# First attention tile of a conv + attention + MoE trunk: the second tile's expert sum moves behind the K/V product and half of Q, and the rows of the third and fourth tiles are gathered once the query weights are there

## The chip, the cores and the metric

One core of one Trainium2 chip runs the whole kernel. The metric is the device time of one execution in microseconds (us), lower is better.

## The reference

The kernel computes two decoder layers over 512 tokens of width 1024, all in float32 (batch 1):

```
layer 0:  x = LN(ALPHA*x + conformer_conv(x))          # 31-wide causal depthwise conv between two products
          x = LN(ALPHA*x + grouped_moe(x))             # 16 experts, top 2 of one group, 1024 -> 512 -> 1024
          k, v = rope(x @ kv_w[:, :256] + ..), x @ kv_w[:, 256:] + ..   # 4 kv heads of 64
layer 1:  q = rope(x @ wq + bq)                        # 16 heads of 64
          x = LN(ALPHA*x + (softmax(q k^T / 8, window 128, one sink a head) v) @ wo + bo)
          x = LN(ALPHA*x + grouped_moe(x))
```

The experts' results are weighted with two gates a token and added to the token's row: `y = sum of gate_j * expert_j(x)`, j = 0, 1.

## The kernel before, in words

The 512 tokens are 4 tiles of 128 tokens (`T = 4`), a tile being [128 partitions x 1024]. The program is written for each engine by hand: a list of instructions that runs in its written order, with semaphores between the lists. Five lists matter here: PE (matrix products and transposes), DVE (vector work, reads the products), ACT (copies out of PSUM, exponentials, and a DMA queue), POOL (`rstd`, the residual, and all indirect DMAs) and SP (the weights' DMA queue).

Between the experts of layer 0 and the attention, each tile goes through the same steps ("combine" in DVE's list, L1499):

- POOL gathers the tile's expert results from DRAM (`xs_dram`), two indirect DMAs of 128 rows of 4 KB each into `yg[l][t][0..1]` (L2102; semaphore `s_yg[t]`, 32 when both have landed). `yg_slots` (L216) says which weight slots hold these rows.
- ACT scales the first of the two with its gate, in place (`gated_y`, L1860, semaphore `s_y0g`).
- DVE adds the second, scaled, to `x` (L1510), adds the first (L1513), and makes the layer norm: statistics (L1215 to L1218, semaphore `s_mv`), a scaling (L1252), and after POOL's `rstd` (`inverse_std`, L2036, one instruction) the last step (L1259, semaphore `s_ln`). `s_ln` reaches `T + 1` when tile 0 is done and `T + 2` when tile 1 is. Tile 0 uses a slightly different sum (L1476, L1482) and no `gated_y`.

The attention runs over the tiles 0 to 3. Its work is cut in units, named kind and tile, which PE makes (`unit`, L1009) and ACT or DVE take (`take`): Xa and Xb are the two halves of the tile's transpose (PE L1024, taken by ACT L1882), KV, Q0 and Q1 the products with the K/V weights and the two halves of the query weights (PE L1032, 16 matmuls each), KT, QTa and QTb the transposes of K and of the two halves of Q. For KV, Q0 and Q1, DVE adds the bias and rotates (L1531 to L1536, L1575 to L1586). W0 and W1 are the output products (PE L1051). Every engine goes through the units in one written order: `first_units` (L408) is Xa, Xb, KV, Q0, Q1, KT, QTa of tile 0, and then for each tile four steps, one for each kv head. In a step stand: the scores (PE L1079), softmax in DVE (`soft`: L1613 to L1624), ACT's exponentials (`exps`: L1892, L1894, eight and one), the normalisation (`normed_probs`: DVE L1631 to L1634), PE's transpose of the probabilities (L1091), ACT's copy (L1904), and the product with V (PE L1105). Between these PE makes the units of the next tile. In the first step of tile 0 the order is, on PE: scores, Xa(1), Xb(1), QTb(0), KV(1), scores of the next head, transposes of the probabilities; on ACT: Xa(1), Xb(1), the exponentials, QTb(0), ...; on DVE: `soft`, combine of tile 2, `normed_probs`, KV(1), ... Tile 3 is combined in the first step of tile 1.

SP loads the K/V weights in slot 0, the query weights in slots 1 and 2 (`s_wq[0]`, `s_wq[1]`), then waits for the last gathered rows (`s_yg[T - 1]`) and for `s_ln`, and loads the output weights in slots 3 and 4. Before the change, the rows of tile 0 lie in the first half of slot 3, those of tile 1 in slot 6 (a part of `arena`, which also holds K and V of the attention), and those of tiles 2 and 3 in slot 5.

The 56 transposes of the identity at L617 do nothing for the result. They fill PE's wait for tile 0.

POOL's list after the layer 0 experts (L2088):

```
for t in range(T):
    if l == 0 and t == 1:
        inverse_std(n)
        for b in range(2):
            pool.wait_ge(s_y[b], 32 * 8)          # the last two experts' rows are in DRAM
    for j in range(2):
        pool.indirect_dma_start(out=yg[l][t][j], ...)
for t in range(l == 0, T):
    inverse_std(n + t)
```

Of the kernel before, what the change touches and what calls it, by code (L numbers as in the profile page):

```python
# [31 lines left out]
T = S // P  # L32
# [49 lines left out]
def trunk(nc, x_in, positions, conv_w1, conv_b1, conv_dw, conv_dwb, conv_ln_g, conv_ln_b,  # L82
# [14 lines left out]
    with ExitStack() as ctx:  # L97
# [3 lines left out]
        def sem(name):  # L101
            return ctx.enter_context(nc.semaphore(name))
# [110 lines left out]
        hT = [view(AT + 1536, 2, P), view(AT + 1792, 2, P), view(8192, 2, P)]  # L213
        slots = [wring[:, i, :] for i in range(6)] + [view(EARLY, KD * F), view(LATE, KD * F), aux[:, 2 * D:6 * D]]
        ring_order = [[1, 2, 3, 6, 7, 4, 5, 0], [5, 0, 1, 2, 3, 4, 6, 7]]
        yg_slots = [((3, 0), (6, 0), (5, 0), (5, 1)), ((7, 0), (7, 1), (5, 0), (5, 1))]  # L216

        QUARTERED = ((1, 4), (1, 5))

# [25 lines left out]
        SUMMED = (1, T)  # L245
# [52 lines left out]
        s_ln = sem("s_ln")  # L298
# [58 lines left out]
        s_wq = [sem(f"s_wq{i}") for i in range(2)]  # L357
# [126 lines left out]
        def _(sp):  # L484
# [36 lines left out]
            def consumed(l, m):  # L521

                e, kind = divmod(m, 3)
                sp.wait_ge(s_dn if kind == 2 else s_gud, E * l + e + 1)
# [37 lines left out]
            sp.dma_start(slot(2, KD), wq_src[:, :, 512:1024]).then_inc(s_wq[1], 16)  # L562
            sp.wait_ge(s_yg[T - 1], 32)
            consumed(0, 3 * E - 5)
            sp.wait_ge(s_ln, T + 1)
            sp.dma_start(slot(3, KD), wo_src[:, :, 0:512]).then_inc(s_wo[0], 16)
            consumed(0, 3 * E - 2)
            sp.dma_start(slot(4, KD), wo_src[:, :, 512:1024]).then_inc(s_wo[1], 16)
# [574 lines left out]
        def _(dve):  # L1143
# [199 lines left out]
            n = 0  # L1343
# [155 lines left out]
            def combine(l, n, tiles):  # L1499

                for t in tiles:
                    if t == 0:
                        add_far(l)
                        add_kept(l)
                        dve.wait_ge(s_rows2, 16 * 2)
                        norm_x(t, n + t, l, 1)
                        continue
                    y0, y1 = yg[l][t]
                    dve.wait_ge(s_yg[t], 32 * (l + 1))
                    own(dve.scalar_tensor_tensor(out=x_sb[:, t, :], in0=y1, scalar=gate_w[:, 1, t:t + 1],  # L1510
                                                 in1=x_sb[:, t, :], op0=ALU.mult, op1=ALU.add))
                    dve.wait_ge(s_y0g, t - SUMMED[l] + 1)
                    dve.tensor_tensor(x_sb[:, t, :], x_sb[:, t, :], y0, ALU.add).then_inc(s_cmb, 1)  # L1513
                    dve.wait_ge(s_cmb, t - SUMMED[l] + 1)
                    norm_x(t, n + t, l, 1)

            experts(0)
            combine(0, n, range(2))
            n += T


# [37 lines left out]
            def take(u, n):  # L1559

                kind, t = u
                if kind == "E":
                    if t == T - 1:
                        bank = full(dve, u)
                        unscaled_logits(1, n + t, ps[:, bank, 0:E], bank_read[bank - 5])
                        first_picks(1, T - 2)
                    route(1, t)
                    return
                if kind[0] in "XDP" or kind in ("KT", "QTa", "QTb") or u == ("R", T - 2):
                    return  # L1570
                bank = full(dve, u)
                if kind == "KV":
                    if t >= 1:
                        full(dve, ("KT", t - 1))
                    dve.tensor_tensor(v_sb[:, t, :], ps[:, bank, KVD:2 * KVD], kvrow[:, KVD:2 * KVD], ALU.add)  # L1575
                    dve.tensor_tensor(k_sb, ps[:, bank, 0:KVD], kvrow[:, 0:KVD], ALU.add
                                      ).then_inc(bank_read[bank - 5], 1)
                    taken(dve, u)
                    own(rotate(t, k_sb.rearrange("p (h d) -> p h d", h=NKV), NKV,
                               (kr[:, :, 0, 0:HH], kr[:, :, 0, HH:HD]), tk))  # L1580
                    dve.tensor_copy(kr[:, :, 1, :], kr[:, :, 0, :]).then_inc(s_kr, 1)
                elif kind in ("Q0", "Q1"):
                    h = int(kind[1])
                    if t >= 1:
                        full(dve, ("QT" + "ab"[h], t - 1))
                    dve.tensor_tensor(q_sb, ps[:, bank, :], bqrow[:, h * 512:(h + 1) * 512], ALU.add  # L1586
                                      ).then_inc(bank_read[bank - 5], 1)
                    taken(dve, u)
                    part = qr[:, 8 * h:8 * h + 8, :]
                    rotate(t, q_sb.rearrange("p (h d) -> p h d", h=8), 8,  # L1590
                           (part[:, :, 0:HH], part[:, :, HH:HD]), tq).then_inc(s_qr, 1)
                elif kind in ("W0", "W1"):
                    h = int(kind[1])
                    dve.wait_ge(s_xb, t + 1)
                    half_x = x_sb[:, t, h * 512:(h + 1) * 512]
                    dve.scalar_tensor_tensor(out=half_x, in0=half_x, scalar=ALPHA, in1=ps[:, bank, :],
                                             op0=ALU.mult, op1=ALU.add).then_inc(bank_read[bank - 5], 1)
                    if h == 1 and t == T - 1:
                        norm_tile(t, n)
                else:  # L1600
                    places(1, t, bank)
                    first_picks(1, t)
# [32 lines left out]
                                  ).then_inc(s_pn, 1)  # L1635

            for u in first_units:
                take(u, n)
            for t in range(T):
                soft(t, 0)  # L1640
# [27 lines left out]
        def _(act):  # L1668
# [18 lines left out]
            for r in range(ROUNDS):  # L1687
                n = min(SHIFTS, CW - SHIFTS * r)
# [171 lines left out]
            def gated_y(l, t):  # L1860

                y0 = yg[l][t][0]
                act.wait_ge(s_yg[t], 32 * (l + 1))
                act.activation(y0, y0, ACT.Copy, scale=gate_w[:, 0, t:t + 1]).then_inc(s_y0g, 1)
# [20 lines left out]
            def exps(t, kh):  # L1885
                m = NKV * t + kh
                lo = 0 if t else P
                act.wait_ge(s_negm, m + 1)
                gq = slice(kh * GQ, (kh + 1) * GQ)
                for i in range(GQ):  # L1890
                    h = kh * GQ + i
                    act.activation(pr[m % 2][:, i, lo:256], pr[m % 2][:, i, lo:256], ACT.Exp,  # L1892
                                   bias=negm[:, h:h + 1], accum_out=den[:, h:h + 1])
                act.activation(exs[:, 1, gq], exs[:, 0, gq], ACT.Exp).then_inc(s_ex, 1)  # L1894
# [19 lines left out]
            for i, u in enumerate(first_units):  # L1914
                take(u)
                if i == 1:
                    for t in range(SUMMED[0], T):
                        gated_y(0, t)
            act.dma_start(resrow, attn_bo[0].partition_broadcast(P)).then_inc(s_rows3, 16)
            norm_rows(1, s_rows3)  # L1920
            for t in range(T):
                for kh, (early, late) in enumerate(fillers(t)):
                    if kh:
                        exps(t, kh)
                    for u in early:
                        take(u)
                    if kh == 0:
                        exps(t, 0)
                    if kh:
                        keep_o(t, kh - 1)  # L1930
                    for u in late:
                        take(u)
                    keep_pt(t, kh)
                    if t == T - 1 and kh < 2:
                        permuted(1, kh)
                if t == T - 1:
                    for u in last_units[0:3]:
                        take(u)
                keep_o(t, NKV - 1)
# [15 lines left out]
        def _(pool):  # L1955
# [78 lines left out]
            def inverse_std(n):  # L2034
                pool.wait_ge(s_mv, n + 1)
                pool.tensor_tensor(rstd[:, n:n + 1], vareps[:, n:n + 1], half[:, :], ALU.pow).then_inc(s_rs, 1)  # L2036
# [51 lines left out]
            def combine(l, n):  # L2088
                stored = in_register(pool, r_pool, pool.snap(g, min_val=1, max_val=4096) * (16 * QUADS))
                for b in range(2):  # L2090
                    pool.wait_ge(s_y[b], 32 * (8 * (l + 1) - l - (l == 0)))
                if l == 0:
                    pool.wait_ge(s_gud, E - 1)
                pool.wait_ge(s_oy, stored)

                for t in range(T):
                    if l == 0 and t == 1:
                        inverse_std(n)
                        for b in range(2):
                            pool.wait_ge(s_y[b], 32 * 8)  # L2100
                    for j in range(2):
                        pool.indirect_dma_start(out=yg[l][t][j], out_offset=None, in_=xs_dram[:, :],  # L2102
                                                in_offset=bass.IndirectOffsetOnAxis(ap=place_i[:, j, t:t + 1], axis=0)
                                                ).then_inc(s_yg[t], 16)
                for t in range(l == 0, T):
                    inverse_std(n + t)

            def number_kept():
# [64 lines left out]
```

## Time and profile before

| | |
|---|---|
| median of 3 runs | 1044.74 us (1037.29, 1044.74, 1045.21) |
| the profiled execution | 1046.18 us, of which the span of the profile is 1044.5 us |
| busy in the span | PE 936.1 us (90%), DVE 455.1, ACT 182.8, POOL 191.4 |
| mean granted TensorE clock | 0.969 of full |
| moved by DMA | 308.71 MB, 296 GB/s over the span |

The profile is of one execution. Times in it are us from the start of the span. The page cuts the span in 40 slices of 26.1 us, and gives the busy share in tenths for each engine and for the 16 DMA engines. The stretch that the change touches is from 500 to 580 us, the 20th to 23rd slice. All sums are made against the profiled execution.

### The profile page before, as it was taken

The numbers are of one execution on the slowest core, as the hardware profiler recorded it, in microseconds if no ns is written. First come the engines' busy times: TensorE is split into PE (matmuls) and PEld (weight loads), VectorE is DVE, ScalarE is ACT, GpSimd is POOL, SyncE is SP. The second block draws the span as 40 slices with busy tenths as digits, with TensorE's granted clock in tenths as the row PEclk, the third lists the DMA queues.
The fourth block names the chain that finished last, engine by engine and source line by source line (L and its number), as shares of the span: only waits on it lengthen the run. The fifth ranks groups of instructions, "written<-read, shape, count | busy, mean of one in ns | idle before, by whom it ended". The sixth has DMA issues, their size and how long they took to land.

```text
span 1044.5 us, 15695 instructions
## 1 busy us (share of the span) xinstructions
PE 936.1 (90%) x6044; PEld 500.4 (48%) x6044; DVE 455.1 (44%) x915; ACT 182.8 (17%) x398; POOL 191.4 (18%) x319
## 2 busy tenths in 40 slices
PE   6999989999999689979989899989999878998994
PEld 4444444557454345534534444454665444544541
DVE  4799983454121011111377586658512211121136
ACT  0100031242111001000032423346311000100100
POOL 1230021023312022100300031002132112212031
PEclk9999999899999899999999899998999989999998
DMA  9995279987999999999880022405879999999982
GB/s 286 376 410 205 72 251 393 378 326 301 365 359 386 396 390 393 391 401 410 325 336 1 1 81 81 161 1 202 300 277 389 371 400 407 371 417 382 416 326 89
DMA packets 75352, 308.71 MB, mean 296 GB/s; under 512 B 9519, under 2 KB 21723, under 8 KB 59130
## 3 DMA queue, kind: packets, MB, share of 16 engines
q1 hardware_dynamic: 37344, 230.32, 57.5%
q10 hardware_dynamic: 27930, 51.14, 13.2%
q0 software_dynamic: 9984, 25.97, 6.9%
q8 instruction: 63, 1.03, 0.4%
q14 instruction: 31, 0.25, 0.1%
HBM read 250.33 MB, written 53.74 MB: 291 GB/s over the span
## 4 chain that ended last, share of the span: by engine, by line
PE 56%; DMA 17%; DVE 15%; issue 7%; ACT 2%; POOL 1%; ACTq 0%; SPq 0%; POOLq 0%; DVEq 0%
PE ps L827 17%; DVE arena L1201 8%; PE ps L837 8%; DMA wring<-in_moe_w_gate_dram 6%; PE ps L722 6%; PE ps L847 4%; DMA arena<-in_moe_w_gate_dram 3%; PE ps L1032 3%; DMA wring<-in_moe_w_up_dram 3%; PE ps L649 3%; PE ps L1051 3%; DMA wring<-in_attn_wq_dram 3%; PE ps L857 2%; PE ps L610 1%; PE ps L1002 1%
## 5 line engine op out<-in xcount | busy, mean ns | idle before, releaser
L827 PE MATMUL ps<-wring,arena 128*64 128x256 f32 x1504 | 177.6, 391 | 24.6 <-DMA wring<-in_moe_w_gate_dram 15.8
L827 PEld LDWEIGHTS ps<-wring,arena 128*64 128x64 f32 x1504 | 109.9, 140 | 86.6 <-DMA wring<-in_moe_w_gate_dram 18.7
L649 PE MATMUL ps<-arena,wring 128*128 128x512 f32 x256 | 110.4, 593 | 1.4 <-DVE arena L1159 1.4
L1407 DVE COPY arena<-ps 128x256 f32<-128x256 f32 x32 | 13.6, 425 | 219.1 <-PE ps L941 202.4
L1201 DVE SCALAR_TENSOR_TENSOR arena<-arena,dwT 128x512 f32<-128x512 f32 x145 | 102.3, 780 | 0.0
L1032 PE MATMUL ps<-wring,arena 128*128 128x512 f32 x192 | 86.3, 604 | 7.0 <-DMA wring<-in_attn_wq_dram 4.0
L837 PE MATMUL ps<-wring,arena 128*64 128x512 f32 x384 | 86.5, 592 | 0.0
L2050 POOL DMA_DIRECT2D arena<-xs_dram x112 | 59.7, 540 | 117.7 <-DVE arena L1386 80.4
L649 PEld LDWEIGHTS ps<-arena,wring 128*128 128x128 f32 x256 | 48.5, 190 | 61.9 <-issue 60.3
L827 PE MATMUL ps<-arena 128*64 128x256 f32 x544 | 65.9, 397 | 9.5 <-DMA arena<-in_moe_w_gate_dram 9.5
L2036 POOL TENSOR_TENSOR rstd<-vareps,half 128x1 f32<-128x1 f32 x20 | 23.8, 1189 | 265.4 <-DVE vareps L1218 265.4
L722 PE MATMUL ps<-wring,arena 128*128 128x512 f32 x128 | 61.3, 634 | 0.5 <-DVE x_sb L1266 0.5
L1032 PEld LDWEIGHTS ps<-wring,arena 128*128 128x128 f32 x192 | 36.2, 193 | 50.2 <-issue 49.3
L1799 ACT ACTIVATE arena<-ps 128x512 f32<-128x512 f32 x32 | 19.1, 597 | 215.4 <-PE ps L837 215.4
L827 PEld LDWEIGHTS ps<-arena 128*64 128x64 f32 x544 | 40.1, 143 | 34.1 <-DMA arena<-in_moe_w_gate_dram 11.5
L1401 DVE TENSOR_TENSOR arena<-arena,ps 128x256 f32<-128x256 f32 x32 | 13.4, 420 | 87.9 <-PE ps L827 87.9
L837 PEld LDWEIGHTS ps<-wring,arena 128*64 128x64 f32 x384 | 27.5, 137 | 45.2 <-issue 41.9
L1051 PE MATMUL ps<-wring,arena 128*128 128x512 f32 x96 | 42.5, 595 | 0.0
L1417 DVE TENSOR_TENSOR arena<-arena,ps 64x256 f32<-64x256 f32 x14 | 5.9, 424 | 79.6 <-ACT arena L1820 79.6
L847 PE MATMUL ps<-wring,arena 128*32 128x256 f32 x608 | 40.2, 380 | 0.0
L722 PEld LDWEIGHTS ps<-wring,arena 128*128 128x128 f32 x128 | 25.3, 204 | 29.9 <-issue 28.9
L2075 POOL COPY arena<-arena 128x256 f32<-128x256 f32 x14 | 5.6, 401 | 177.4 <-DMA arena<-xs_dram 115.7
(251 smaller groups left out, 1145.0 us busy)
## 6 DMA issues: line engine op xcount, KB each, us to landing
wring<-in_moe_w_gate_dram SPq DMA_DIRECT2D x23, 2048.0 KB, 25.0
wring<-in_moe_w_up_dram SPq DMA_DIRECT2D x23, 2048.0 KB, 19.5
wring<-in_moe_w_down_dram SPq DMA_DIRECT2D x23, 2048.0 KB, 22.9
xs_dram<-zero ACTq DMA_DIRECT2D x2, 16384.0 KB, 50.3
arena<-in_moe_w_gate_dram SPq DMA_DIRECT2D x9, 2048.0 KB
arena<-in_moe_w_up_dram SPq DMA_DIRECT2D x8, 2048.0 KB
arena<-in_moe_w_down_dram SPq DMA_DIRECT2D x6, 2048.0 KB
xs_dram<-arena ACTq DMA_DIRECT2D x60, 128.0 KB, 8.9
```

Source lines behind the costliest of these rows:

```text
L649: last = pe.matmul(ps[:, 2 * (c % 4) + h, :], w[:, k, h, (c % 2) * P:(c % 2) * P + P], xT[:, k, :], start=(k == 0), stop=(k == KD - 1))
L722: last = pe.matmul(ps[:, 4 + h, :], hc[t % 2][:, c, :], slot(4 + c // 4, 4)[:, c % 4, h * 512:(h + 1) * 512], start=(c == 0), stop=(c == K ...
L827: mm = pe.matmul(ps[h * CAP:(h + 1) * CAP, bank, 0:256], act[:, k, :], w[:, k, h * 256:(h + 1) * 256], start=(k == 0), stop=(k == KD - 1))
L837: mm = pe.matmul(ps[h * CAP:(h + 1) * CAP, bank, :], act[:, j % 2, (j // 2) * CAP:(j // 2 + 1) * CAP], w[:, j, h * 512:(h + 1) * 512], sta ...
L847: mm = pe.matmul(ps[q * XROWS:(q + 1) * XROWS, bank, 0:256], xgxT[:, k, :], gate_up[i][:, k, h * 256:(h + 1) * 256], start=(k == 0), stop= ...
L857: mm = pe.matmul(ps[q * XROWS:(q + 1) * XROWS, bank, 0:D // QUADS], hTx[:, at:at + XROWS], w[:, j, q * (D // QUADS):(q + 1) * (D // QUADS) ...
L1032: last = pe.matmul(ps[:, bank, :], xTt[:, k, :], slot(at, KD)[:, k, :], start=(k == 0), stop=(k == KD - 1))
L1051: last = pe.matmul(ps[:, bank, :], oT[t % 2][:, k, :], slot(3 + h, KD)[:, k, :], start=(k == 0), stop=(k == KD - 1))
L1201: dve.scalar_tensor_tensor(out=acc, in0=hpad[:, c, k:k + S], scalar=dwT[:, c, k:k + 1], in1=acc, op0=ALU.mult, op1=ALU.add).then_inc(s_tap, 1)
L1799: act.activation(ysb[b], ps[:, 4, :], ACT.Copy).then_inc(s_yc, 1)
L2036: pool.tensor_tensor(rstd[:, n:n + 1], vareps[:, n:n + 1], half[:, :], ALU.pow).then_inc(s_rs, 1)
L2050: pool.dma_start(where[q * QROWS:(q + 1) * QROWS, :, :], xs_tiles[q, :, bass.ds(n, 1), :, :]).then_inc(signal, 16)
```

## The change

Five edits, which hang together:

1. DVE combines tile 1 not before `first_units` but within them, after it has taken Q0 and before it takes Q1.
2. POOL issues the gathers of tile 1 as before, then makes tile 1's `rstd`, then waits until the second half of the query weights has landed (`s_wq[1]`), and only then issues the four gathers of tiles 2 and 3.
3. ACT scales tile 1's rows after Xb as before, but tile 2's after all of `first_units`, and tile 3's after the first exponentials of tile 0.
4. The rows of tile 1 are gathered to the second half of slot 3 in place of slot 6.
5. SP's load of the output weights into slot 3 waits for `s_ln` at `T + 2` (tile 1 done) in place of `T + 1`.

```diff
-        yg_slots = [((3, 0), (6, 0), (5, 0), (5, 1)), ((7, 0), (7, 1), (5, 0), (5, 1))]
+        yg_slots = [((3, 0), (3, 1), (5, 0), (5, 1)), ((7, 0), (7, 1), (5, 0), (5, 1))]
...
             consumed(0, 3 * E - 5)
-            sp.wait_ge(s_ln, T + 1)
+            sp.wait_ge(s_ln, T + 2)
             sp.dma_start(slot(3, KD), wo_src[:, :, 0:512]).then_inc(s_wo[0], 16)
...
             experts(0)
-            combine(0, n, range(2))
+            combine(0, n, range(1))
...
             for u in first_units:
+                if u == ("Q1", 0):
+                    combine(0, n - T, range(1, 2))
                 take(u, n)
...
             for i, u in enumerate(first_units):
                 take(u)
                 if i == 1:
-                    for t in range(SUMMED[0], T):
-                        gated_y(0, t)
+                    gated_y(0, 1)
+            gated_y(0, 2)
             act.dma_start(resrow, attn_bo[0].partition_broadcast(P)).then_inc(s_rows3, 16)
             norm_rows(1, s_rows3)
...
                     if kh == 0:
                         exps(t, 0)
+                        if t == 0:
+                            gated_y(0, 3)
...
                 for t in range(T):
+                    if l == 0 and t == 2:
+                        inverse_std(n + 1)
+                        pool.wait_ge(s_wq[1], 16)
                     if l == 0 and t == 1:
                         inverse_std(n)
...
-                for t in range(l == 0, T):
+                for t in range(2 if l == 0 else 0, T):
                     inverse_std(n + t)
```

## Rows read from the trace of the kernel before

**Rows 1.** The page: PE's busy time, and the DMA engines' share in 40 slices.

```profile
PE 936.1 (90%) x6044; PEld 500.4 (48%) x6044; DVE 455.1 (44%) x915; ACT 182.8 (17%) x398; POOL 191.4 (18%) x319
...
DMA  9995279987999999999880022405879999999982
```

**Rows 2.** The chain that ended last, from 496 us: start, us, what.

```profile
496.54 6.14 DMA wring<-xs_dram,place_i
...
503.79 27.40 DMA wring<-in_attn_wq_dram
```

**Rows 3.** Timeline of PE: start, us, line, instructions merged, idle before and its releaser.

```profile
513.40 13.11 PE L1032 MATMUL ps<-wring,arena 128*128 128x512 f32 x30 [0.77 <-ACT arena L1882]
...
524.63 2.74 PE L1032 MATMUL ps<-wring,arena 128*128 128x512 f32 x6
531.32 8.80 PE L1032 MATMUL ps<-wring,arena 128*128 128x512 f32 x16 [3.96 <-DMA wring<-in_attn_wq_dram]
...
544.56 7.10 PE L1032 MATMUL ps<-wring,arena 128*128 128x512 f32 x16 [0.43 <-ACT arena L1882]
...
553.41 0.66 PE L1091 MATMUL ps<-ident,arena 128*128 128x128 f32 x4 [1.10 <-DVE arena L1634]
...
602.15 7.13 PE L1051 MATMUL ps<-wring,arena 128*128 128x512 f32 x16
```

**Rows 4.** Windows: PE busy, granted clock, DMA share, GB/s.

```profile
527.00:529.00 2.00, 0.37 (x1) 1.00 1.04 410
529.00:531.00 2.00, 0.00 (x0) 1.00 0.35 138
...
533.00:535.00 2.00, 2.00 (x3) 0.50 0.81 272
...
582.00:584.00 2.00, 2.00 (x12) 0.52 0.00 0
```

**Rows 5.** Timeline of DVE, tile 1's sum to tile 0's first probabilities.

```profile
523.94 1.28 DVE L1510 SCALAR_TENSOR_TENSOR x_sb<-arena,gate_w,x_sb 128x1024 f32<-128x1024 f32 x1 [12.53 <-DMA arena<-xs_dram,place_i]
...
528.08 0.15 DVE L1218 TENSOR_SCALAR vareps<-mv 128x1 f32<-128x1 f32 x1
...
529.96 1.28 DVE L1259 SCALAR_TENSOR_TENSOR x_sb<-x_sb,rstd,aux 128x1024 f32<-128x1024 f32 x1 [0.53 <-POOL rstd L2036]
...
533.86 0.68 DVE L1586 TENSOR_TENSOR arena<-ps,aux 128x512 f32<-128x512 f32 x1
...
536.63 0.42 DVE L1536 TENSOR_TENSOR arena<-arena 128x256 f32<-128x256 f32 x1
...
543.28 0.68 DVE L1613 SCALAR_TENSOR_TENSOR arena<-ps,mask 128x512 f32<-128x512 f32 x1
...
545.07 1.28 DVE L1510 SCALAR_TENSOR_TENSOR x_sb<-wring,gate_w,x_sb 128x1024 f32<-128x1024 f32 x1
...
552.66 0.69 DVE L1634 TENSOR_TENSOR arena<-arena,rden 128x512 f32<-128x512 f32 x1
```

**Rows 6.** Timeline of POOL: tile 3's last gather, tile 1's rstd.

```profile
520.33 0.95 POOL L2102 DMA_INDIRECT wring<-xs_dram,place_i  x1 [0.30 <-issue]
528.32 1.53 POOL L2036 TENSOR_TENSOR rstd<-vareps,half 128x1 f32<-128x1 f32 x1 [7.04 <-DVE vareps L1218]
```

**Rows 7.** Timeline of ACT and its DMA queue (ACTq), up to the first exponentials.

```profile
531.67 1.15 ACT L1864 ACTIVATE wring<-wring,gate_w 128x1024 f32<-128x1024 f32 x1 [2.51 <-DMA wring<-xs_dram,place_i]
...
541.04 0.39 ACTq L1919 DMA_DIRECT2D aux<-in_attn_bo_dram  x1
...
541.93 0.45 ACTq L1696 DMA_DIRECT2D aux<-in_ln_b_dram  x1
543.22 1.08 ACT L1882 ACTIVATE arena<-ps 128x512 f32<-128x512 f32 x2 [1.54 <-PE ps L1024]
```

**Rows 8.** An indirect DMA's issue on POOL beside DVE work, in the last tile.

```profile
749.48 1.80 POOL L2044 DMA_INDIRECT xs_dram<-x_sb,place_i  x1 [0.96 <-DVE place_i L1317]
```

**Rows 9.** Timeline of DVE at that place.

```profile
749.10 1.28 DVE L1252 SCALAR_TENSOR_TENSOR x_sb<-x_sb,mv,aux 128x1024 f32<-128x1024 f32 x1
```

## The prediction

> **What bounds the kernel now.** The page comes first: PE is busy for 90% of the span, and the DMA engines are nearly full except in slices 21 to 26, the attention [rows 1]. So around 500 to 530 us two things are tight at once: PE waits for what it needs, and every byte in flight delays every other. The chain that ended last goes there from a gather (496.54 us, 6.14 us long) straight into the load of the second half of the query weights, issued at 503.79 and landed 27.40 us later, at 531.19 [rows 2]. PE's timeline shows what that costs: KV and Q0 of tile 0 run from 513.40 without a gap to 524.63 + 2.74 = 527.37, PE then stands still for 3.96 us, and Q1 takes 8.80 us where the same 16 matmuls take 7.10 at 544.56 [rows 3]. The windows say why: behind the gap the granted clock falls to 0.50, the lower of its two levels, 1.2 of 2.4 GHz [rows 4]. So the late weights cost 3.96 + 1.70 = 5.7 us at this place. From 544.56 the list goes on through KV(1), the scores and the transposes of the first probabilities at 553.41, which waited 1.10 us for DVE [rows 3]. After this point the four steps of each tile hang on one another through PE, DVE and ACT, and the expert weights of layer 1 are loaded as the attention frees its slots, into a DMA stream that is full to the end [rows 1]. I therefore carry a shift of 553.41 to the end one to one.
>
> **What the held-back gathers free.** Four gathers of 0.52 MB, 2.1 MB, leave the stream ahead of the query weights. At 410 GB/s, the rate just before the drain [rows 4], that is 5.1 us, so the weights land at about 526, before PE has finished Q0 at 527.4 (the drain itself, 410 then 138 GB/s, moves along). Q1 then starts at 527.4, at full clock, and ends at 534.5. The gain at this place is the 5.7 us from above.
>
> **What moves on DVE.** Tile 1's sum and norm take 523.94 to 529.96 + 1.28 = 531.24, 7.3 us, and the K/V unit follows, to 533.86, 2.6 us; the Q0 unit goes on to 536.63 + 0.42 = 537.05, 3.2 us [rows 5]. After the change the K/V unit lies under the Q0 product and costs nothing. The Q0 unit starts at 527.4 and ends at 530.6, tile 1's sum and norm end at 537.9, and the Q1 unit (3.2) ends at 541.1. The softmax of head 0, from 543.28 to 545.07 before [rows 5], can be over at 542.9. That is 2.2 us earlier. DVE's order alone has thus already eaten 3.5 of the 5.7 us. KT and QTa need only the K/V and Q0 units, so PE and ACT are through them some 3 us after 534.5.
>
> **Where the gathers go.** POOL now makes tile 1's rstd before it issues them, so they wait for DVE, not for the weights. From the start of tile 1's sum to its variance are 528.08 + 0.15 - 523.94 = 4.3 us [rows 5], and rstd takes 1.53 after a tenth [rows 6]: 530.6 + 4.3 + 1.6 = 536.5. The weights landed at 526, so that second wait is free. Issues cost 0.95 us and 0.30 between them [rows 6]. The first falls on DVE's last norm step (from 536.6, 1.28 us, two inputs in SBUF). The nearest row is the issue at 749.48, beside the same kind of step at 749.10: 1.80 us in place of 0.95 [rows 8, 9]. I take that for the first issue only: 536.8 to 538.6, second from 538.9. A second gather after a pause needed 6.14 us [rows 2], so tile 2's rows land at 538.9 + 6.1 = 545.0, tile 3's 2.5 us later. Bounds: with no slowing of the issue and a quicker landing 543.4; with both issues slowed and a landing a microsecond slower 547.
>
> The Trainium skill ("DMA: Bandwidth & Descriptors", the section on the anatomy of one DMA from GpSimd) gives about 2.0 us plus the bytes at 436 GB/s for such a DMA. By it the second gather would land some 4.2 us after its issue begins instead of 6.1, an estimate from its figures, and the sum below would be 1.9 us smaller. The row here is longer and decides. The skill's "SBUF — State Buffer" ("Who interferes with whom") says that a DVE instruction with two SBUF inputs and a GpSimd instruction that reads SBUF exclude each other for the whole of an instruction; the 1.80 us issue agrees, and taken literally, a blocked second issue would add up to about half a microsecond.
>
> **Who waits for tile 2's rows.** Two engines. ACT meets `gated_y(0, 2)` right after QTa, at about 537, and stands there until 545.0. Before, it scaled the last rows at 531.67, when it had nothing else to do [rows 7]. Behind it are queued the three DMA issues of the bias and norm rows (541.04 to 541.93 + 0.45 = 1.34 us), the copies Xa(1) and Xb(1) (1.08 us) [rows 7], and all exponentials. The issues run beside the scaling (1.15 us), so the copies start at 546.3 and end at 547.4, and PE can start KV(1) 0.26 us later, as it did at 544.56 after the copies' end at 544.30 [rows 3, 7]: at 547.7, which is 3.1 us later than before. PE itself is there long before. It has made Xa(1), Xb(1) and QTb(0) by 542 and has had little since 535. A wait like that costs clock: 4 us of standing still took 1.70 us from Q1 [rows 3, 4]. I take 1.7 here as well. KV(1) ends at 547.7 + 7.1 + 1.7 = 556.5, and with 0.7 for the scores (553.41 - 1.10 - 551.66) the transposes of the probabilities come at 557.2. The second waiter is DVE: tile 2's sum and norm start at 545.0 instead of 545.07 and so end when they did, and the probabilities are ready at 553.3 as before (552.66 + 0.69) [rows 5], 4 us before PE wants them. The 1.10 us that PE waited for them is gone.
>
> **The sum.** 557.2 - 553.4 = +3.8 us. In terms of the steps: +3.1 for KV(1)'s start, +1.7 clock, -1.1 for the wait that is absorbed, and 0.1 of rounding. The 5.7 us at Q1 are spent before KV(1), because KV(1) doesn't wait for Q1 any more but for ACT.
>
> **Edits with no cost.** Tile 3's rows (landed about 547.5) are scaled after the exponentials, about 550, 1.15 us more of ACT; the QTb copy behind it is wanted for the third head only. The output weights' loads move from 531.7 to about 547.5 and, 4.2 MB at 410 GB/s, land by some 558; the first product with them is at 602.15 [rows 3]. `s_ln` at `T + 2` comes at 537.9 and doesn't end that wait. The other half of slot 3 holds the same bytes as slot 6 would. Without that cover of over 40 us the load's 10 us would show in full; nothing here comes near.
>
> **The rivals.**
> (a) *The gathers are in time, faster.* If tile 2's rows landed before DVE is through head 0's softmax at 542.9, ACT would be free, and the transposes would start when DVE is ready, 2.2 us earlier than before. For: the gathers meet an empty DMA stream. Against: 542.9 leaves 4.0 us from the second issue, and no row shows a landing under 6. It gives 1042.6, and is the most that can be gained: DVE's order alone forbids more.
> (b) *Nothing reaches the end.* Any of the later waits (PE's wait for DVE at the end of tile 0, the full DMA stream of layer 1) takes up the shift: 1044.7. Against: both are started by the same list.
> (c) *The clock stays low, slower by over 1%.* Between 535 and 547 PE has only some 3 us of transposes and scores. In the sparse stretch after tile 0's last head the clock was still at 0.52 from 582 to 584 [rows 4]. If PE were at 1.2 GHz through KV(1) and the work after it, as long as each product only follows short waits, KV(1) and Q0(1) would cost 7.1 us more each in place of 1.7: +3.1 - 1.1 + 14.2 = +16 us, 1061. It decides from the point where a full product no longer brings the clock back; Q1's 8.80 us speak against it, since the clock was back within the product. With only KV(1) wholly slow it is +9.1, 1053.8.
>
> **How the numbers follow.** The profiled execution took 1046.18 us and the median is 1044.74; I put the shift on the median: 1044.7 + 3.8 = 1048.5. The forecast's own ends are 543.4 for the landing with no clock lost (KV(1) at 546.1, transposes at 553.9: +0.5, 1045.2) and 547 with 3.5 us of clock lost (+7.7, 1052.4). Chances: forecast 0.66, (a) 0.14, (b) 0.12, (c) 0.08, of which half stays within 1%. The runs of before lie 8 us apart (1037.29 to 1045.21), so about 1% (10.4 us) is what a measurement can tell from no change, and a median can fall low by itself; with that and (a) the low end is 1041, the high end 1053. Faster by over 1%: 0.03, for a low median on top of (a). Slower by over 1%: 0.06. Within 1%: 0.91.
>
> **What the profile after would show.** Right: Q1 of tile 0 starting at 527 to 528 with no wait and taking 7.1 us; POOL's four gathers from about 537; ACT's longest wait, 6 us or more, at L1864 for a DMA; KV(1) at 547 to 548, released by ACT's copy. Wrong: an ACT wait under 3 us there (then (a)), the gathers waiting for the weights rather than for rstd, PE still idle before Q1 (the stream isn't what held the weights), or KV(1)'s shift not found again in the start of layer 1's experts (then (b)).

## The result and the profile after

The changed kernel took 1050.32 us (median of 20 runs) against 1044.33 for the kernel before (20 runs): ratio 1.0048, 95% interval 1.0034 to 1.0063, or 5.0 us slower on 1044, between 3.6 and 6.6. (The two medians lie 6.0 us apart; what follows goes by the ratio and its interval.) The forecast was +3.8 us. Run again later beside the kernel before, the ratio was 1.0046 (1.0023 to 1.0069), and the kernel before against itself gave 0.9992 (0.9967 to 1.0018).

Every execution reaches the first KV product at another time (513.40 in the profile of before, 510.52 here), so the spans of two profiles, 1044.5 and 1045.6, can't be set against each other. I count from the start of that product instead, written as +.

PE's timeline after the change, to be read against [rows 3]:

```profile
510.52 20.84 PE L1032 MATMUL ps<-wring,arena 128*128 128x512 f32 x48 [0.78 <-ACT arena L1884]
...
533.06 0.71 PE L1079 MATMUL ps<-arena 64*128 64x128 f32 x8 [0.83 <-ACT arena L1884]
535.65 1.16 PE L1024 MATMUL ps<-ident,x_sb 128*128 128x128 f32 x8 [1.87 <-DVE arena L1586]
538.25 1.09 PE L1044 MATMUL ps<-ident,arena 128*128 128x128 f32 x4 [1.44 <-DVE arena L1536]
543.36 9.26 PE L1032 MATMUL ps<-wring,arena 128*128 128x512 f32 x16 [4.03 <-ACT arena L1884]
...
553.20 0.66 PE L1091 MATMUL ps<-ident,arena 128*128 128x128 f32 x4
```

KV, Q0 and Q1 are one row of 48 matmuls with no gap: the weights are there. Then PE waits four times, the last time and longest for ACT's copies before KV(1), which starts at +32.84 and takes 9.26 us instead of 7.1. The 1.10 us wait for DVE at L1091 is gone. ACT's timeline says why (its L1866 is the scaling, L1884 the copies), with its DMA queue's issues among it, against [rows 7]:

```profile
540.46 1.15 ACT L1866 ACTIVATE wring<-wring,gate_w 128x1024 f32<-128x1024 f32 x1 [7.54 <-DMA wring<-xs_dram,place_i]
540.46 0.39 ACTq L1921 DMA_DIRECT2D aux<-in_attn_bo_dram  x1
540.89 0.44 ACTq L1697 DMA_DIRECT2D aux<-in_ln_g_dram  x1
541.36 0.62 ACTq L1698 DMA_DIRECT2D aux<-in_ln_b_dram  x1
542.03 1.09 ACT L1884 ACTIVATE arena<-ps 128x512 f32<-128x512 f32 x2 [0.42 <-issue]
```

ACT stood 7.54 us for tile 2's rows; behind it the three issues, then the copies, then KV(1). DVE's and POOL's timelines, against [rows 5, 6]:

```profile
527.65 1.28 DVE L1510 SCALAR_TENSOR_TENSOR x_sb<-wring,gate_w,x_sb 128x1024 f32<-128x1024 f32 x1
...
533.66 1.34 DVE L1259 SCALAR_TENSOR_TENSOR x_sb<-x_sb,rstd,aux 128x1024 f32<-128x1024 f32 x1 [0.53 <-POOL rstd L2040]
534.92 0.68 DVE L1586 TENSOR_TENSOR arena<-ps,aux 128x512 f32<-128x512 f32 x1
...
540.46 1.28 DVE L1510 SCALAR_TENSOR_TENSOR x_sb<-wring,gate_w,x_sb 128x1024 f32<-128x1024 f32 x1 [0.56 <-DMA wring<-xs_dram,place_i]
```

```profile
532.02 1.53 POOL L2040 TENSOR_TENSOR rstd<-vareps,half 128x1 f32<-128x1 f32 x1 [18.64 <-DVE vareps L1218]
533.74 0.99 POOL L2109 DMA_INDIRECT wring<-xs_dram,place_i  x1 [0.18 <-issue]
535.03 0.94 POOL L2109 DMA_INDIRECT wring<-xs_dram,place_i  x1 [0.30 <-issue]
```

POOL's 18.64 us wait before the rstd is for DVE, not for the weights, which needed 22.8 us from issue to landing here and were there at +13.2. The gathers follow right behind it, and the rows are there 5.43 us after the second issue began. The windows of the changed kernel, all engines (the stretch, its length, then the busy time of PE, PEld, DVE, ACT and POOL, then clock, DMA share, GB/s), show the clock at the lower level from before KV(1) starts to well within it, against [rows 4]:

```profile
541.00:543.00 2.00, 0.00 (x0) 0.00 (x0) 1.97 (x2) 1.58 (x3) 0.00 (x0) 0.50 0.94 356
...
545.00:547.00 2.00, 2.00 (x4) 0.76 (x3) 1.47 (x2) 2.00 (x8) 1.37 (x1) 0.50 0.97 305
547.00:549.00 2.00, 2.00 (x5) 0.82 (x4) 1.70 (x4) 0.69 (x2) 0.00 (x0) 0.82 0.93 320
549.00:551.00 2.00, 2.00 (x6) 0.95 (x5) 0.00 (x0) 0.00 (x0) 0.00 (x0) 1.00 1.03 397
```

The prediction named the start of layer 1's experts as the place to look for the shift again. PE's first products there (L827), in the changed kernel and then in a second profile of the kernel before (c1 below), whose first KV product starts at 511.04:

```profile
760.66 10.58 PE L827 MATMUL ps<-wring,arena 128*64 128x256 f32 x96 [0.80 <-issue]
```

```profile
755.44 10.58 PE L827 MATMUL ps<-wring,arena 128*64 128x256 f32 x96 [0.90 <-issue]
```

That is +250.1 against +244.4; the other two profiles have +250.6 (changed) and +247.0 (before). So the changed kernel reaches this place 3 to 6 us later, and the end of the span 3.5 to 5.0 us later (+535.1 and +536.1 against +531.1 and +531.6).

### The profile page after: what moved, and what is told of

The parts are those of the page before. It is cut to its first block, busy times and chain, and to the rows that moved or that the text cites. A ratio compares the mean times of both kernels' runs of the same rounds, so it can differ in the third digit from the quotient of the medians.

```text
span 1045.6 us, 15695 instructions
## 1 busy us (share of the span) xinstructions
PE 933.1 (89%) x6044; PEld 498.9 (48%) x6044; DVE 455.2 (44%) x915; ACT 182.2 (17%) x398; POOL 190.8 (18%) x319
## 4 chain that ended last, share of the span: by engine, by line
PE 57%; DVE 16%; DMA 14%; issue 8%; ACT 2%; POOL 1%; ACTq 0%; SPq 0%; POOLq 0%; DVEq 0%
PE ps L827 17%; DVE arena L1201 8%; PE ps L837 8%; DMA wring<-in_moe_w_gate_dram 6%; PE ps L722 6%; DMA wring<-in_moe_w_up_dram 5%; PE ps L847 4%; PE ps L1051 3%; PE ps L1032 3%; PE ps L649 3%; PE ps L857 2%; PE ps L610 1%; DMA wring<-xs_dram,place_i 1%; PE ps L1091 1%; PE ps L941 1%
## 5 line engine op out<-in xcount | busy, mean ns | idle before, releaser
L827 PE MATMUL ps<-wring,arena 128*64 128x256 f32 x1504 | 178.8, 393 | 26.2 <-DMA wring<-in_moe_w_gate_dram 15.4
L827 PEld LDWEIGHTS ps<-wring,arena 128*64 128x64 f32 x1504 | 110.2, 141 | 88.9 <-DMA wring<-in_moe_w_gate_dram 18.3
L2040 POOL TENSOR_TENSOR rstd<-vareps,half 128x1 f32<-128x1 f32 x20 | 23.8, 1188 | 269.3 <-DVE vareps L1218 269.3
L827 PE MATMUL ps<-arena 128*64 128x256 f32 x544 | 64.6, 391 | 8.9 <-DMA arena<-in_moe_w_gate_dram 8.3
L1032 PEld LDWEIGHTS ps<-wring,arena 128*128 128x128 f32 x192 | 36.5, 194 | 50.0 <-issue 44.7
L827 PEld LDWEIGHTS ps<-arena 128*64 128x64 f32 x544 | 39.5, 141 | 32.8 <-DMA arena<-in_moe_w_gate_dram 10.1
```

What stands on the lines that cost most here:

```text
L827: mm = pe.matmul(ps[h * CAP:(h + 1) * CAP, bank, 0:256], act[:, k, :], w[:, k, h * 256:(h + 1) * 256], start=(k == 0), stop=(k == KD - 1))
L1032: last = pe.matmul(ps[:, bank, :], xTt[:, k, :], slot(at, KD)[:, k, :], start=(k == 0), stop=(k == KD - 1))
```

## The experiments

Twelve runs were made in three groups (e1 to e4; e5 to e8; c1, c2, e9 and e10), each group on one chip beside the kernel before. The table collects, from each one's profiled execution, four marks of PE's timeline in us from the start of the first KV product, and the ratio of all its runs. "First transposes" are the first ones at L1091, the mark at which the prediction closed its sum.

| kernel | wait before Q1 | KV(1): start, length | first transposes | KV(2): start, length | ratio (95% interval) |
|---|---|---|---|---|---|
| before, first profile | 3.96 | +31.16, 7.10 | +40.01 | +71.75, 7.11 | 1 |
| before again (c1) | 2.12 | +27.63, 7.11 | +36.47 | +68.03, 7.11 | 0.9992 (0.9967, 1.0018) |
| changed | 0 | +32.84, 9.26 | +42.68 | +73.38, 7.11 | 1.0048 (1.0034, 1.0063) |
| changed again (c2) | 0 | +32.41, 9.15 | +42.14 | +73.62, 9.03 | 1.0046 (1.0023, 1.0069) |
| e1 no hold | 2.70 | +28.22, 7.10 | +37.59 | +69.51, 9.02 | 0.9998 (0.9973, 1.0022) |
| e2 hold by weights only | 0 | +28.56, 9.01 | +38.15 | +69.62, 9.03 | 0.9988 (0.9970, 1.0006) |
| e3 ACT's copies first | 0 | +28.61, 9.63 | +39.66 | +71.13, 8.91 | 1.0001 (0.9980, 1.0022) |
| e4 changed, fillers | 0 | +33.27, 7.03 | +40.88 | +72.54, 8.66 | 1.0006 (0.9988, 1.0024) |
| e5 old DVE order | 0 | +28.54, 7.75 | +36.95 | +68.65, 7.11 | 0.9993 (0.9969, 1.0017) |
| e6 hold only | 0 | +32.00, 7.11 | +39.68 | +70.94, 7.11 | 1.0030 (1.0003, 1.0057) |
| e7 = e2, fillers | 0 | +28.16, 7.03 | +37.60 | +68.57, 7.11 | 0.9965 (0.9941, 0.9990) |
| e8 = e6, fillers | 0 | +31.42, 7.10 | +39.11 | +68.40, 7.10 | 0.9981 (0.9959, 1.0002) |
| e9 = e5, fillers | 0 | +27.69, 7.11 | +36.58 | +65.87, 7.11 | 0.9944 (0.9922, 0.9965) |
| e10 = before, fillers | 1.97 | +28.40, 7.10 | +37.27 | +66.55, 7.10 | 0.9955 (0.9936, 0.9974) |

The marks are those of one execution each, the ratio is that of all. Some profiled executions were shorter than their kernel's median (changed 1047.26 us with a median of 1050.32, c2 1046.26 with 1048.04, e5 1037.52 with 1041.50, e6 1043.27 with 1046.88), some longer (e3 1049.25 with 1045.24, e4 1049.37 with 1047.24, e7 1042.71 with 1039.89). A difference of 2 or 3 us between two rows' marks therefore says little about their ratios: e3 and e6 have the same mark, and 1.0001 and 1.0030.

### e1: the changed kernel without the hold

```diff
-                    if l == 0 and t == 2:
-                        inverse_std(n + 1)
-                        pool.wait_ge(s_wq[1], 16)
...
-                for t in range(2 if l == 0 else 0, T):
+                for t in range(l == 0, T):
```

> The changed kernel with the gathers of tiles 2 and 3 issued right behind tile 1's, as before the change (tile 1's rstd after them, no wait for the weights). Theory A (the held-back rows hold ACT, and ACT holds KV(1)): ACT scales tile 2's rows without a wait, but the query weights are late again (27 us from issue to landing), Q1 waits some 4 us and takes 8.8 us, DVE's second-tile sum fits under that wait, and KV(1) starts 31 us after the first KV product, as in the kernel before: ratio 0.999 to 1.001. Rival B (DVE's new order or the later output weights cost the time, not the held-back rows): still 4 to 5 us slower than before, ratio 1.004 to 1.005.

Ratio 0.9998, so the whole loss, to within 2.8 us, goes with the hold (the wait and the rstd ahead of it); DVE's new order, the slot and SP's later load cost nothing that shows. Its PE timeline:

```profile
525.84 7.11 PE L1032 MATMUL ps<-wring,arena 128*128 128x512 f32 x16 [2.70 <-DMA wring<-in_attn_wq_dram]
...
537.38 7.10 PE L1032 MATMUL ps<-wring,arena 128*128 128x512 f32 x16
```

Two things were not as expected: the wait before Q1 is 2.70 us, not 4, and Q1 runs at full speed. That led to c1.

### e2: hold by the weights alone

```diff
                     if l == 0 and t == 2:
-                        inverse_std(n + 1)
                         pool.wait_ge(s_wq[1], 16)
...
-                for t in range(2 if l == 0 else 0, T):
+                for t in range(l == 0, T):
```

> The changed kernel with POOL waiting for the query weights alone before it gathers tiles 2 and 3; tile 1's rstd comes after the gathers. Theory A: the gathers go out about 10 us earlier (near the end of the Q0 product), tile 2's rows land before ACT has copied QTa, so both the 5.7 us at Q1 and the early copies are kept; KV(1) starts some 3 us earlier than before, the transposes of the first probabilities wait for DVE and come 2 us earlier: ratio 0.997 to 0.999. Rival B (DVE's order is what costs): no better than the changed kernel, 1.004 to 1.005. Rival C (any shift here is lost in later clock dips): 1.000 within the interval.

Ratio 0.9988, inside theory A's range; the interval holds rival C's 1.000 as well and ends 3.5 us short of rival B's number. POOL's first held gather and PE's KV(1):

```profile
524.25 0.95 POOL L2108 DMA_INDIRECT wring<-xs_dram,place_i  x1 [10.33 <-DMA wring<-in_attn_wq_dram]
```

```profile
539.12 1.09 PE L1044 MATMUL ps<-ident,arena 128*128 128x128 f32 x4 [1.07 <-DVE arena L1536]
540.00 9.01 PE L1032 MATMUL ps<-wring,arena 128*128 128x512 f32 x16
```

The gathers go out at +12.8 instead of +23.2, ACT never waits for them, and KV(1) starts 4.3 us sooner than in the changed kernel. But it is slow again (9.01), behind two small waits for DVE (1.82 and 1.07 us): the weights come early, and then PE waits for DVE.

### e3: ACT's copies ahead of its wait

```diff
-            gated_y(0, 2)
             act.dma_start(resrow, ...)
...
                     if kh == 0:
+                        if t == 0:
+                            gated_y(0, 2)
                         exps(t, 0)
```

> The changed kernel with one instruction of ACT moved: the scaling of tile 2's rows stands behind the copies Xa(1) and Xb(1) instead of before them; POOL holds the gathers as in the change. Theory A: KV(1) no longer waits for the rows and starts about 29 us after the first KV product (2 us earlier than before, 4 earlier than in the changed kernel) and at full clock; then DVE's sum of tile 2, which still waits for the rows, sets the first transposes, at the same time as before: ratio 0.999 to 1.001. Rival B: 1.004 to 1.005, since ACT's wait was not what mattered.

Ratio 1.0001, as theory A says, with the gathers held as late as in the change. This is the direct test of the place of the loss: one instruction of ACT moved behind two copies (and behind the three DMA issues), and the loss is gone, to within 2.3 us.

```profile
539.37 9.63 PE L1032 MATMUL ps<-wring,arena 128*128 128x512 f32 x16
...
550.42 0.66 PE L1091 MATMUL ps<-ident,arena 128*128 128x128 f32 x4 [0.78 <-DVE arena L1634]
```

KV(1) starts at +28.61 as expected, but takes 9.63 us, not 7.1, and the transposes then wait 0.78 us for DVE, which waited for the rows. Full clock was a wrong expectation. The rows themselves came later than in the change, 6.77 us after the second issue began instead of 5.43. ACT's queue, POOL and ACT:

```profile
532.51 0.39 ACTq L1920 DMA_DIRECT2D aux<-in_attn_bo_dram  x1
```

```profile
535.27 0.94 POOL L2110 DMA_INDIRECT wring<-xs_dram,place_i  x1 [0.30 <-issue]
```

```profile
542.04 1.15 ACT L1866 ACTIVATE wring<-wring,gate_w 128x1024 f32<-128x1024 f32 x1 [4.33 <-DMA wring<-xs_dram,place_i]
```

In e3 the bias and norm rows, 1.5 MB, are issued just ahead of the gathers, because ACT doesn't wait; in the change they are issued after the landing. That they share the stream and cost the 1.3 us fits the two traces, but no run tests it alone.

### e4: fillers before KV(1)

```diff
+                    if t == 0 and kh == 0:
+                        idle(3, 14)
                     for u in late:
+                        if u == ("KV", 1):
+                            idle(3, 36)
                         unit(u)
```

> The changed kernel with 50 more transposes of the identity on PE, 14 before QTb(0) and 36 before KV(1), where PE stands still; they write a PSUM bank that nobody reads then. They keep the granted clock up and change nothing else. Theory A: KV(1) starts when it did (33 us after the first KV product) but takes 7.1 us in place of 9.3, so some 2 us of the loss go: ratio 1.002 to 1.003. Rival D (the clock is no part of it, or the extra work delays the units as much as it gives): 1.005.

Ratio 1.0006, better than either number. KV(1) does what was forecast:

```profile
541.72 4.09 PE L617 MATMUL ps<-ident 128*128 128x128 f32 x36
545.64 7.03 PE L1032 MATMUL ps<-wring,arena 128*128 128x512 f32 x16
```

It starts at +33.27, no sooner, and takes 7.03 us: the clock alone is 2.2 us of KV(1) in the change. The ratio gained 4.4 us, twice as much, with an interval of nearly 2 us on each side; where the rest comes from, the profiles can't show, since e4's is of an execution 2.1 us slower than its median and that of the change of one 3.1 us faster.

### e5 and e6: the hold with DVE's old order

e5 is the changed kernel with DVE's combine of tile 1 put back ahead of the first units. e6 is the kernel before plus the hold, with the rstd behind the gathers:

```diff
e5:  -            combine(0, n, range(1))          e6:  +   if l == 0 and t == 2:
     +            combine(0, n, range(2))               +       pool.wait_ge(s_wq[1], 16)
     -   if u == ("Q1", 0):                             +   # gated_y(0, 2) behind first_units,
     -       combine(0, n - T, range(1, 2))             +   # gated_y(0, 3) behind exps(0, 0), as in the change
```

> The changed kernel with DVE's order alone put back: tile 1 is combined ahead of the first units. POOL still makes tile 1's rstd and then waits for the weights before it gathers tiles 2 and 3. Theory A (the time of the landing against ACT's and DVE's need decides): rstd comes about 15 us after the first KV product's start, the gathers go out at some +15.5 and tile 2's rows land at +23, when ACT has just copied QTa; Q1 starts without a wait; KV(1) starts at about +28.5, the transposes of the first probabilities at +37.5, 2.5 us before the kernel before: ratio 0.997 to 0.999. Rival E (the old order alone was all that made the change slow, or the hold does harm by itself): 1.000 or more.

> The kernel before plus the hold alone: POOL waits for the query weights before it gathers tiles 2 and 3 (tile 1's rstd after them), ACT scales them later as in the change; DVE's order, slots and SP as before. Theory A: Q1 starts without a wait, the rows land before anyone needs them: transposes of the first probabilities 2.5 to 3 us before the kernel before, ratio 0.997 to 0.999. Rival C (a lead here is lost again in the clock dip behind tile 0's last head): 1.000.

e5 gave 0.9993, whose interval holds both the forecast and no change, and e6 1.0030, which was forecast faster and is slower. In e5 KV(1) and the first transposes come when they were forecast (+28.5 and +37.5); wrong was the +40 that they were compared with. The weights are early and PE waits elsewhere, for DVE's Q0 unit, which ends at +23.8:

```profile
531.73 0.63 PE L1044 MATMUL ps<-ident,arena 128*128 128x128 f32 x4 [2.48 <-DVE arena L1536]
...
544.76 0.66 PE L1091 MATMUL ps<-ident,arena 128*128 128x128 f32 x4
```

The wait for the weights (2.12 us in c1) has turned into one for DVE of about the same size, and the first transposes (+36.95) are no earlier than in the kernel before (+36.47 in c1). In e6 the held gathers stand in POOL's list ahead of tile 1's rstd, and DVE waits 2.79 us for it where it waited 0.53 [rows 5]. POOL, then DVE:

```profile
524.22 0.95 POOL L2106 DMA_INDIRECT wring<-xs_dram,place_i  x1 [0.30 <-issue]
525.19 0.59 POOL L2038 TENSOR_TENSOR rstd<-vareps,half 128x1 f32<-128x1 f32 x1
```

```profile
525.88 1.28 DVE L1259 SCALAR_TENSOR_TENSOR x_sb<-x_sb,rstd,aux 128x1024 f32<-128x1024 f32 x1 [2.79 <-POOL rstd L2038]
```

So putting the rstd ahead of the held gathers, as the change does, protects DVE in the old order (KV(1) at +28.54 in e5 against +32.00 in e6) and harms ACT in the new one (+32.84 against +28.56 in e2). The ratios of e5 and e6 overlap, and the two also differ in the slot of tile 1's rows and in SP's wait.

### e7 to e10: fillers behind tile 0's last head, and the two controls

Each version without fillers there waits 3.67 or 3.68 us at the end of tile 0 for DVE's last softmax, and the scores, transposes and often KV(2) behind it run slowly. e8, e9 and e10 fill that wait:

```diff
                     if kh + 1 < NKV:
                         scores(t, kh + 1)
+                    if t == 0 and kh == NKV - 1:
+                        idle(3, 32)
                     turn(t, kh)
```

e10 is the kernel before with this alone, e8 is e6 with it, e9 is e5 with it and 20 fillers before QTa of tile 0, and e7 is e2 with it and 15 and 9 fillers around Xa(1) and Xb(1).

> The changed kernel with POOL waiting for the weights alone, as in the earlier run, and with 56 filler transposes of the identity on PE: 15 before Xa(1), 9 before QTb(0), 32 before tile 0's last transposes of probabilities. Theory A with the clock's part: KV(1) and KV(2) take 7.1 us each in place of 9.0, which KV(1) gives only up to DVE's probabilities (about 1 us) and KV(2) in full (2 us): ratio 0.995 to 0.997. Rival D (fillers give no time): 0.999 as without them.

> The kernel before plus the hold alone, with 32 filler transposes on PE before tile 0's last transposes of probabilities, where PE stands still for 3.7 us in every version. Theory A with the clock's part: KV(2) at 7.1 us in place of 9.0 and the scores and transposes before it at full clock too, 2 to 4 us less than without the fillers: ratio 0.994 to 0.997. Rival D: no change against the version without fillers.

> The changed kernel with DVE's order put back (held gathers behind tile 1's rstd) and 52 fillers on PE: 20 before QTa of tile 0, 32 before tile 0's last transposes of probabilities. Theory A: the first transposes at about +37 us, KV(2) at +67 to +68 in place of the 68.7 without fillers, later stretch at full clock: ratio 0.995 to 0.997, the best of all, with the weights-only version with fillers. Rival D: 0.999, as without fillers.

> The kernel before with 32 fillers on PE before tile 0's last transposes of probabilities and nothing else. Tells how much of the fillers' versions is owed to them alone. Theory A: the scores, transposes and KV(2) behind the 3.7 us wait run at full clock, 2 us: ratio 0.998, about half of what the versions with hold and fillers gain. Rival G (the fillers are all of it): 0.996.

> The kernel before, unchanged: the control that says how far a ratio of this size can be trusted, and a second look at the wait before Q1. Theory A: ratio within 0.998 to 1.002; the wait before Q1 differs between executions (4.0 us and a slow product in the first profile, 2.7 and a full-speed one in the run without the hold), so the first transposes come 37.5 to 40 us after the first KV product. Rival F (the profile of before was typical): 40 us again.

> The changed kernel, unchanged, beside the others on one chip. Theory A: transposes of the first probabilities 42 to 43.5 us after the first KV product, ratio 1.003 to 1.006. If the ratio comes out under 1.002, the first comparison was partly chance.

e10 gave 0.9955 (4.7 us faster), e9 0.9944 (5.8 us), e7 0.9965, e8 0.9981. e8 gained less than forecast, e7's ratio lies in its range, and e9 and e10 came out faster than theirs. c2 came as expected and so did c1's ratio, but c1's mark (37.5 to 40 forecast) was earlier still. The two best can't be told apart: no run shows that the hold adds anything to what the fillers give, as rival G says. Against the same kernel without fillers, e8 and e9 are 5.1 us faster and e7 2.4 us. In e7 KV(1) ran at full clock, but then PE waited 1.76 us for DVE and the next product was the slow one:

```profile
549.82 1.04 PE L1091 MATMUL ps<-ident,arena 128*128 128x128 f32 x4 [1.76 <-DVE arena L1640]
550.65 8.38 PE L1032 MATMUL ps<-wring,arena 128*128 128x512 f32 x16
```

PE's timeline of e10, and behind it that of the kernel before again (c1):

```profile
566.69 3.66 PE L617 MATMUL ps<-ident 128*128 128x128 f32 x32
570.52 0.66 PE L1091 MATMUL ps<-ident,arena 128*128 128x128 f32 x4 [0.17 <-DVE arena L1636]
...
572.45 1.13 PE L1079 MATMUL ps<-arena 64*128 64x256 f32 x8
573.51 1.16 PE L1024 MATMUL ps<-ident,x_sb 128*128 128x128 f32 x8
575.60 7.10 PE L1032 MATMUL ps<-wring,arena 128*128 128x512 f32 x16 [0.93 <-ACT arena L1884]
```

```profile
527.13 7.11 PE L1032 MATMUL ps<-wring,arena 128*128 128x512 f32 x16 [2.12 <-DMA wring<-in_attn_wq_dram]
...
547.51 0.66 PE L1091 MATMUL ps<-ident,arena 128*128 128x128 f32 x4 [1.09 <-DVE arena L1634]
...
571.72 1.11 PE L1091 MATMUL ps<-ident,arena 128*128 128x128 f32 x4 [3.67 <-DVE arena L1634]
...
574.57 2.08 PE L1079 MATMUL ps<-arena 64*128 64x256 f32 x8
576.58 1.54 PE L1024 MATMUL ps<-ident,x_sb 128*128 128x128 f32 x8
579.07 7.11 PE L1032 MATMUL ps<-wring,arena 128*128 128x512 f32 x16 [0.94 <-ACT arena L1882]
```

From tile 0's last transposes to the end of KV(2) are 12.18 us in e10 (582.70 - 570.52) and 14.46 in c1 (586.18 - 571.72); in c2 and e1, where KV(2) fell under the low clock too, 16.3 and 16.7. So the fillers give 2.3 us at this place against c1 (2.5 against the first profile, where it took 14.63) and up to 4.5 where KV(2) is slow, which no profile of the kernel before shows. The measured 4.7 us (2.7 to 6.7) is shown as the fillers' gain; where the half of it beyond 2.3 us arises is not.

In c1, the kernel before, PE waits 2.12 us before Q1 and Q1 takes 7.11 us. The first transposes come at +36.47, 3.5 us sooner than in the profile on which the prediction rests. e10 has the same list up to there and comes at +37.27. The changed kernel came at +42.68 and +42.14. By c1, e10, the change and c2 the mark differs by some 5.5 us between the kernels, and the time by 5.0. One execution doesn't carry its mark to the end like that: the two profiles of the kernel before differ by 3.5 us at the mark, by 2.6 at layer 1's experts, and at the end of the span the one that was ahead is 0.5 us behind.

## Why the prediction was right

The direction and the mechanism held; that the size came out as near as 1.2 us is in part luck, since two errors cancel (below). Step by step, in us from the first KV product (513.40 in the prediction's terms):

- **Weights early, Q1 without a wait**: landing forecast at +12.6, measured +13.2; end of Q1 forecast at +21.1, measured +20.84.
- **The gathers wait for DVE's tile 1**: rstd done at +23.1 forecast, +23.03 measured. The wait for the weights was free.
- **The issue slowed beside DVE**: mis-sized. I took 1.80 us for the first from a single row; it took 0.99 beside the same kind of step (533.66, 1.34 us), so the 0.85 us didn't come. In c2, e3 and e4 the first held issue took 0.99 as well, and so did the kernel before's first gather behind a pause, at 514.02, with DVE idle beside it, so no slowing by DVE shows. The row that I took, at 749.48, was also of another kind, a scatter of `x_sb` and not a gather. The Trainium skill's rule ("SBUF — State Buffer", "Who interferes with whom") is one for a GpSimd instruction that reads SBUF; that the issue of a gather is one, no run here shows, and what made the 1.80 us stays open.

```profile
514.02 0.99 POOL L2102 DMA_INDIRECT arena<-xs_dram,place_i  x1 [4.00 <-DMA xs_dram<-arena]
```

- **The landing**: 6.1 us from the second issue was too long, DVE and ACT had the rows after 5.43 (5.16 in c2, 5.05 in e4, but 6.77 in e3). The Trainium skill's formula ("DMA: Bandwidth & Descriptors", the anatomy of one DMA from GpSimd) would have given 4.2, an estimate and too short. With the issue this puts the landing at +29.9 against +31.6.
- **ACT holds KV(1)**: 2.90 us from landing to KV(1), forecast 2.7; start +32.84 against +34.3, early by about what the landing was early. e3 shows that this is where the loss is: with the copies first, no loss is left (0.1 us, between -2.1 and 2.3).
- **The clock**: 1.7 us forecast, 2.2 and 2.1 measured (9.26 and 9.15 against 7.1), and e4 takes them back. Rival (c) needed the low clock to outlast a full product; the next one took 7.03 us in both profiles of the change.
- **The wait for DVE's probabilities absorbed**: as forecast.
- **The page's DMA row** is low in slices 22 to 28, not 21 to 26 as the prediction reads it; no term rests on that.

So the changed kernel's first transposes were forecast at +43.8 and came at +42.1 to +42.7. The other end of the difference was off the other way: I took +40.01 for the kernel before, from one execution in which the weights needed 27.4 us. In c1 and e10 they needed 25.6 and 25.8 us, the wait before Q1 was 2.1 and 2.0 us, Q1 kept full clock, and the mark came at +36.5 and +37.3. The "5.7 us at this place" was 2 us in those, and KV(1)'s start moved by 4.0 to 5.2 us, not by 3.1. The two errors, 1.4 us too late after and some 3 us too late before, partly cancel, which leaves +3.8 where 5.0 was measured. Why the weights land 1.7 us apart in two executions of one kernel stays open.

Rival (a), a gain with 2.2 us as its most, is refuted for the changed kernel (the landing came at +29.9, while DVE's softmax was done at +29.4). Its condition was also the wrong one: a landing 0.6 us earlier would have met it and still left ACT, free since +22.4, standing for 7 us; by the prediction's own steps 542.9 gives KV(1) at 545.6 and no gain. The rows must be there when ACT has copied QTa. What (a) promised was nearly tested by e2, which has the rows in time: 0.9988, at best 3 us faster. Rival (b) is out as well: the loss of 5.0 us (3.6 to 6.6) is there at the end, and at layer 1's experts. That a shift of the mark reaches the end one to one is not shown: e3's and e4's marks lie 2 to 4 us behind those of c1 and e10, and their ratios are 1.0001 and 1.0006.

What I had wrong in the experiments was worth more than the forecast. e5 and e6 were forecast to gain 1 to 3 us from early weights; e5 shows no gain clear of the noise (0.7 us, between -1.8 and 3.2), and e6 lost 3. The wait for the query weights had cover: in the old order DVE sums tile 1 and takes KV under it, and when it goes, DVE is late next by about the same (2.48 us in e5).

## What to carry to other kernels

A transfer that is held back to free bandwidth must be asked who stands in line behind its consumer: here ACT's wait for rows that only DVE needed early held two unrelated copies and through them PE, and moving the wait behind the copies removed the 5 us, to within 2.3. Before removing a wait of a few us, look at what the other engines do under it, and look at more than one execution: the wait that the change attacked was 4 us in one profile and 2.0 to 2.7 in three others. Where PE must stand for 3 to 4 us in front of dense work, try some 30 transposes of the identity into a free bank: here 32 of them took the place of a 3.67 us wait, left 0.17 of it, and were worth 4.7 us (2.7 to 6.7), about as much as the change lost.

## What was not expected of the hardware

- After the same 3.67 us wait, the product that follows ran at full clock in some executions (KV(2) 7.11 us: before, c1, changed, e5, e6) and largely under the lower level in others (9.02, 9.03, 9.03: e1, e2, c2; 8.91 and 8.66: e3, e4), with the same list of instructions ahead of it in changed and c2. With fillers it was 7.10 to 7.11 in all four.
- Short work between short waits didn't hold the clock here. In e2 and e3, PE had only waits of under 2 us with short transposes and scores between them, and the product behind them still took 9.0 and 9.6 us.
- Of two gathers issued into an empty DMA stream, the second had landed 5.1 to 5.4 us after its issue began (changed, c2, e4), and 6.8 us after it in e3, where 1.5 MB had been issued just before. Issued beside the weights, tile 1's needed 8.6 us (523.94 against an issue at 515.31 in the first profile).
